# Stick-breaking attention on one core: the score products' key tile without its zero halves

## What is computed

```python
z = jnp.einsum('bqkgd,bskd->bkgqs', qb, kf)            # scores, 64 numbers a head
log_1m_beta = jnp.where(mask, jax.nn.log_sigmoid(-z), 0.0)
rev = lax.cumsum(log_1m_beta, axis=4, reverse=True)    # suffix sums over the keys
excl = jnp.concatenate([rev[..., 1:], jnp.zeros_like(rev[..., :1])], axis=-1)
a = jnp.where(mask, jnp.exp(jax.nn.log_sigmoid(z) + excl), 0.0)
o = jnp.einsum('bkgqs,bskd->bqkgd', a, vf)
```

## Time and profile before

| | us |
|---|---|
| median of 3 runs | 1886.32 |
| lowest, highest | 1879.72, 1889.54 |
| the profiled execution, its own time | 1886.43 |
| its span, first to last instruction | 1884.6 |
| PE busy | 1769.6 |
| DVE busy | 1009.6 |
| ACT busy | 864.7 |
| POOL busy | 89.9 |

### The profile page before, as it was taken

One profiled execution on the slowest core, in us unless ns is written; L12 is line 12 of the kernel. 1 busy time (PEld: TensorE's weight loads), 2 busy tenths in 40 slices (PEclk: granted clock), 3 DMA queues, 4 the chain that ended last, 5 costly groups with the idle time before them and its releaser, 6 DMA issues.

```text
span 1884.6 us, 22494 instructions
## 1 busy us (share of the span) xinstructions
PE 1769.6 (94%) x8544; PEld 1459.7 (77%) x8544; DVE 1009.6 (54%) x1351; ACT 864.7 (46%) x1221; POOL 89.9 (5%) x114
## 2 busy tenths in 40 slices
PE   7968779999997999998999999999999999799997
PEld 5758668888885688886888887888878888468886
DVE  4674536545435555545554556555455545655553
ACT  4532115543437555435443563544354444855442
POOL 0022400000011000000000100000000000000000
PEclk9989799999988999998999999999999999999999
DMA  7320005455521044554455654555545555225552
GB/s 269 151 91 1 1 24 179 178 188 190 232 91 45 23 168 178 189 201 145 178 180 204 252 181 155 180 187 190 201 162 196 182 197 198 71 90 179 178 193 97
DMA packets 41164, 291.87 MB, mean 155 GB/s; under 512 B 4832, under 2 KB 4992, under 8 KB 6528
## 3 DMA queue, kind: packets, MB, share of 16 engines
q1 hardware_dynamic: 39968, 282.91, 41.6%
q0 software_dynamic: 1120, 7.88, 1.3%
HBM read 289.73 MB, written 1.05 MB: 154 GB/s over the span
## 4 chain that ended last, share of the span: by engine, by line
PE 89%; DVE 7%; ACT 2%; issue 1%; POOL 1%; DMA 0%; SPq 0%; POOLq 0%; DVEq 0%; ACTq 0%
PE ps L577 25%; PE ps L579 25%; PE ps L578 25%; PE ps L591 3%; PE ps L1077 1%; PE ps L928 1%; DVE w_lo L1617 1%; PE ps L915 1%; PE ps L925 1%; PE ps L1006 1%; PE ps L774 1%; PE ps L1090 1%; PE ps L1103 0%; ACT w_hi L1169 0%; PE ps L956 0%
## 5 line engine op out<-in xcount | busy, mean ns | idle before, releaser
L1617 DVE TENSOR_TENSOR w_lo<-raw,w_hi 128x1024 fp32r<-128x1024 f32 (+1 forms) x532 | 619.4, 1206 | 488.9 <-ACT w_hi L1169 485.1
L1169 ACT ACTIVATE w_hi<-raw 128x1024 fp32r<-128x1024 f32 (+1 forms) x532 | 527.0, 1040 | 508.3 <-PE ps L579 496.2
L577 PE MATMUL ps<-w_hi,h_hi 128*128 128x512 f32 x1424 | 570.0, 400 | 20.7 <-DVE w_lo L1617 13.2
L579 PE MATMUL ps<-w_hi,h_lo 128*128 128x512 f32 x1424 | 560.1, 393 | 0.0
L578 PE MATMUL ps<-w_lo,h_hi 128*128 128x512 f32 x1424 | 559.4, 393 | 0.0
L577 PEld LDWEIGHTS ps<-w_hi,h_hi 128*128 128x128 f32 x1424 | 270.5, 190 | 81.9 <-issue 18.4
L579 PEld LDWEIGHTS ps<-w_hi,h_lo 128*128 128x128 f32 x1424 | 270.2, 190 | 58.3
L578 PEld LDWEIGHTS ps<-w_lo,h_hi 128*128 128x128 f32 x1424 | 271.0, 190 | 53.5
L577 PE MATMUL ps<-w_hi,hid_hi 128*128 128x512 f32 x672 | 263.2, 392 | 0.0
L579 PE MATMUL ps<-w_hi,hid_lo 128*128 128x512 f32 x672 | 261.7, 389 | 0.0
L578 PE MATMUL ps<-w_lo,hid_hi 128*128 128x512 f32 x672 | 261.5, 389 | 0.0
(11 more groups left out here) (278 smaller groups left out, 1268.8 us busy)
## 6 DMA issues: line engine op xcount, KB each, us to landing
raw<-in_stream SPq DMA_DIRECT2D x266, 1024.0 KB, 4.8
ns_w<-in_ns_w POOLq DMA_DIRECT2D x1, 4096.0 KB, 14.4
ln_rows<-in_ln_rows POOLq DMA_DIRECT2D x2, 1024.0 KB, 9.9
const<-in_const SPq DMA_DIRECT2D x1, 1202.0 KB, 14.3
x_sb<-in_x SPq DMA_DIRECT2D x2, 512.0 KB, 7.7
out<-x_sb SPq DMA_DIRECT2D x2, 512.0 KB, 3.1
row<-in_fin_rows SPq DMA_DIRECT2D x1, 512.0 KB, 18.7
row<-in_fin_rows POOLq DMA_DIRECT2D x1, 512.0 KB, 4.0
```

The lines of the kernel that those rows point to most:

```text
L577: pe.matmul(bank[tt], a_hi[:, k_at + k, rows], hi, start=(k == 0), stop=False)
L579: done = pe.matmul(bank[tt], a_lo[:, k_at + k, rows], hi, start=False, stop=(k == q.kt - 1))
L1169: act.activation(w_hi[:, static % 2, part], raw[:, static % RING, part], ACT.Copy).then_inc(hi_ready, 1)
L1617: dve.tensor_tensor(w_lo[:, static % 2, part], raw[:, static % RING, part], w_hi[:, static % 2, part].bitcast(F32), ALU.subtract).then_inc ...
```

## The change

`sb_kt` loses its `par` dimension, and with it the zeros. ACT copies all 128 partitions of the transposed keys at once; the keys stand in both halves already. The score product of `par` 0 takes rows 0 to 63 of keys and queries, that of `par` 1 rows 64 to 127. The memset, its semaphore and ACT's wait for it are gone. Results and PSUM banks are as before.

```diff
-        sb_kt = view("sb_kt", [P, 2, 4, T], 16 * KB)
+        sb_kt = view("sb_kt", [P, 4, T], 16 * KB)
...
                     for par in range(2):
-                        done = pe.matmul(ps[:, 2 * (u % 2) + par, 0:256], sb_kt[:, par, g, kt * P:(kt + 1) * P],
-                                         sb_qt[:, 2 * g:2 * g + 2, qt * P:(qt + 1) * P], start=True, stop=True)
+                        rows = slice(64 * par, 64 * par + 64)
+                        done = pe.matmul(ps[:, 2 * (u % 2) + par, 0:256], sb_kt[rows, g, kt * P:(kt + 1) * P],
+                                         sb_qt[rows, 2 * g:2 * g + 2, qt * P:(qt + 1) * P], start=True, stop=True)
...
                 def store_t(first):
 
-                    act.wait_ge(sb_kz, 1)
...
                         else:
-                            for par in range(2):
-                                rows = slice(64 * par, 64 * par + 64)
-                                done = act.activation(sb_kt[rows, par, 2 * n:2 * n + 2, :].rearrange("p f t -> p (f t)"),
-                                                      ps[rows, 4 + n % 2, :], ACT.Copy)
+                            done = act.activation(sb_kt[:, 2 * n:2 * n + 2, :].rearrange("p f t -> p (f t)"),
+                                                  ps[:, 4 + n % 2, :], ACT.Copy)
...
                     pool.tensor_copy(sb_kd[:, :, :, half, :], heads).then_inc(sb_copied, 1)
-                pool.memset(sb_kt[:, :, :, :].rearrange("p r g t -> p (r g t)"), 0.0).then_inc(sb_kz, 1)
```

More of the change, by code:

```diff
@@ L443, in build @@
         sb_copied = sem("sb_copied")
-        sb_kz = sem("sb_kz")
         sb_in = sem("sb_in")
```

## The result

| | before | after |
|---|---|---|
| median of 20 runs each, us | 1885.78 | 1889.86 |
| lowest, highest, us | 1877.35, 1889.54 | 1885.05, 1891.32 |
| ratio, 95% interval | | 1.0024 (1.0015 to 1.0033) |
| the profiled execution, us | 1886.43 | 1890.67 |
| its span, us | 1884.6 | 1888.9 |

The account below looks back on a forecast made before the run. It took TensorE, busy 94% of the span, to bound the kernel, and DVE's work the edited mixer's rounds. -1.1 us on the path plus 3.4 for the clock gave +2.3 on 1886.32: 1888.7 us, range about 1880 to 1894.

Parts of the forecast that it names:

- What goes without a price: Ahead of the mixer: removed memset wait and ACT's key copies, done 1.2 us earlier, give 0 on the path.
- The row halves: Score products on rows 0 to 63 and 64 to 127 run side by side: a unit costs 0.43 us, not 0.86.
- the step of L786: Pace of the value products on two column halves, eight records in 1.08 us, assumed for the score products.
- The rival that they don't overlap: Score products: the row halves don't run side by side; 0 to -0.5 us, about 1886 us, chance 0.10.
- The switch of shape: Array going from full to half shape at the scores: 0.14 us each in five places, 0.7 us if not hidden.
- What of it the path sees: DVE's five waits for scores in the mixer vanish: 1.1 us less; DVE is what is late next.
- What the freed time costs: PE's longer idle gaps in the mixer bring two more low-clock stretches at 1.7 us each: +3.4 us.
- The first gap: PE's idle time between the scores and the first suffix sum: 2.98 us before, 3.4 us forecast.
- one slow round for each gap over 3 us: Mixer rounds: each PE gap over 3 us brings one round at low clock; two more, 1.7 us each.
- The clock doesn't mind: Rival: PE's longer mixer gaps pass at full clock, -1.1 us remain, 1885.3 us; chance 0.30.
- Low throughout: Rival: clock stays low for the whole mixer, +11.4 us, 1897.8 us; chance 0.05.
- The 9.4 us: 0.5% of the whole kernel's time, taken as about what a measurement can tell from no change.

Follow-up runs that it names:

- filled changed kernel: The changed kernel with 5, 5, 3, 3 and 3 unread products of constants in PE's gaps ahead of the first five rounds' suffix sums: 1881.43 us, ratio 0.9967.
- filled kernel before: The kernel before with 4, 4, 2, 2 and 3 unread products of constants in PE's gaps: 1883.05 us, ratio 0.9987.
- six profiles with whole products: Profiles with full-array score product gaps: kernel before with 0, 2, 4, 6 products ahead, full-array products with new copies (1884.17 us), 64-row pairs issued twice (1886.51 us).
- four places: Either kernel with 0, 2, 4 or 6 products of constants ahead of the key transposes: before 1885.78, 1883.97, 1887.92, 1888.70 us; changed 1889.86, 1887.73, 1890.28, 1893.22 us.
- the rows alone: The kernel before with score products on 64 rows each, but par dimension, memset and four half-height copies kept: 1886.56 us, ratio 1.0006.
- the shifts: Both kernels with 2, 4 or 6 products of constants ahead of the key transposes: before 1883.97, 1887.92, 1888.70 us; changed 1887.73, 1890.28, 1893.22 us.
- the copies alone: The changed kernel with full-array score products, keeping no memset and two full-height key copies: 1884.17 us, ratio 0.9994.

## Why the prediction was right

**What goes without a price** was right by its own steps. ACT ended its key copies at 1605.2 (1605.3 worked out), waited 4.12 us for PE (3.9), and the mixer didn't come earlier.

**The row halves**: I took the step of L786, and eight records took 1.14 us where those of L786 take 1.08. The rival that they don't overlap is out. The switch of shape was priced at 0.14 us and costs about 0.2: scores start 0.96 us behind the carry sums in the filled changed kernel, 0.86 in the filled kernel before, and the first two records take 0.48 us where later ones take 0.38, which holds up the next two by 0.1. In the rounds it stayed hidden.

```profile
1644.75 0.49 PE L764 MATMUL ps<-sb_qt,sb_kt 64*128 64x256 f32 x2
```

**What of it the path sees** was named right and sized low. DVE does become the next in line: in the filled kernel, the list of its waits for 1616 to 1661 has none for scores left:

```profile
DVE sb_s L1862 <- PE ps L778: 4.1, 4, 1.0
DVE sb_s L1862 <- PE ps L776: 4.0, 8, 0.6
DVE w_lo L1624 <- ACT w_hi L1179: 0.7, 1, 0.7
```

But the gain is about 1.5 us, not 1.1. The wait list counted only DVE's idle time. A round went from 6.35 to 6.12 us, 0.23 where the wait was 0.17, in three rounds, and at the start the masking of the fourth unit came 0.77 us earlier against the transposes where the waits add up to 0.59: 1.46 in all. (The mixers' lengths differ by 1.6, because the first score product starts 0.1 us later behind the transposes, at the switch of shape.) The surplus over the waits is overlap on DVE: where the input is there, an instruction starts before the one ahead of it has ended. In the filled kernel the masking of the first round starts 0.05 us before the end of the subtraction (L1862 at 1625.88 for 0.69, masking at 1626.52), where before it came 0.17 us behind it.

**What the freed time costs** is the term that decided, and it was sized low by over a third, 3.4 us against 5.5. The first gap came out as worked out, 3.4 us. The second was 2.66 instead of 3.3, because the scores ahead of it ran at half clock, and the clock was low again all the same. So the rule that I counted by, one slow round for each gap over 3 us, picked the right two rounds without being the right rule: the second and third slow rounds followed 2.66 and 2.02 us. Its premise, that gaps of 2.98 and 2.64 us pass, came from one execution; in the six profiles with whole products they were followed by slow sums in half the cases. I took two more slow rounds at 1.7 us; there were three more, and two of them made DVE wait 0.5 us for its scores besides. The chain after has, for the scores of a round's first unit at half and at full clock, and for the carry sums of the last slow round:

```profile
1627.97 1.18 PE ps L764 x4
...
1635.70 1.18 PE ps L764 x4
...
1644.82 0.66 PE ps L764 x4
...
1660.71 0.94 PE ps L776 x2
```

The sum: L774 over 1.98 us by 1.80, 1.08, 1.62 and 1.64, L776 by 0.07, the first unit's scores of two rounds by 0.5 each over 0.66, is 7.2 us; less the 1.7 of the slow round before, 5.5; less the 1.5 won, 4.0. Measured between the two traces, from the second block's transposes to the end of the mixer: 4.1 us. The forecast's form, minus the path gain plus the clock, is right, with -1.5 and +5.5 in place of -1.1 and +3.4. That 1888.7 came so near to 1889.9 is in part luck: the errors of the two terms went opposite ways, and the count of slow rounds differs from one execution to the next, from one to three in the kernel before and from three to four in the changed one at its four places.

**Rivals.** "The clock doesn't mind" is out. "Low throughout" didn't happen: after each slow round of the profiled run the clock came back. The 9.4 us named as what a measurement can tell from no change was far too coarse: 20 runs of each tell 4.1 us from nothing. The Trainium skill (TensorE: Matmul & The Clock Gate, section What's actually happening) calls the lower rate the default, which activity lifts; what filling did agrees, with a granted clock of 1.00 from 1619.6 us on. The Trainium skill (TensorEngine Tiling (Array Packing), section Key Properties) says that a change of tiling mode drains the array; the rows show some 0.2 us at the switch, which nothing waited for in the rounds.

Not shown: what decides between a gap of 2.05 us that passes and one of 2.02 us that doesn't; why the rows alone, with the same products, are mostly some 3 us faster than the changed kernel; and why the profiled run and the median differ at the shifts.

## What to carry to other kernels

Before taking work off an engine that waits for others within its stage, ask what its clock does in the gaps: here TensorE gave up 0.75 us of work a round, most of it work that nobody waited for, and paid up to 1.8 us on the suffix sums that everybody waits for. Don't read from one execution which gaps the clock lets pass: here the same gaps passed in some and not in others. A saving off the path is worth its overlap with another engine's wait and no more, and that can be read ahead of time in the wait list (1.1 us here, about 1.5 in truth). Where such gaps are short and fixed, products of constants in them are a cheap test of whether the clock is what one pays for, and here also gave the fastest version measured.

## What the runs showed of the hardware that I had not expected

- With nothing changed in its own work, the mixer of the kernel before took 47.2 to 50.4 us, through one to three slow rounds, and 51.8 in the kernel with the copies alone. Each is one execution. Of the profiles taken at the shifts, a pair could have shown the changed mixer anything from 1.2 us shorter (49.2 against 50.4) to 4.3 longer (51.5 against 47.2).
- A gap of 2.02 us on PE was followed by half clock and one of 2.05 us wasn't. The same gap of 2.98 us ahead of the first suffix sums was followed by sums at full clock in two profiles and by slow ones in three, with as much work of PE ahead of it in the mixer. So the length of the last gap alone doesn't tell.
- Two f32 products on the two row halves start together although each is two records of the same half in a row. At half clock a record of L764 took 0.63 us before and the next started 0.43 us behind it, so that two in a row span 1.06 us; after the change the first two span 0.80. Together they still take 0.17 us longer than one did before, the price of the switch of shape in it. The trace doesn't name the half that a record uses; that a pair is one of each half is inferred from the rows before, where the two records of a product never start together. All records of the line in the kernel before (least, median, longest ns) and two in a row there:

```profile
L764 PE MATMUL ps<-sb_qt,sb_kt x48: 379/379/634, 1616.4 to 1649.0; 128*128 128x256 f32 x48
1616.78 1.06 PE L764 MATMUL ps<-sb_qt,sb_kt 128*128 128x256 f32 x2
```

The first two in the changed kernel:

```profile
1616.59 0.80 PE L764 MATMUL ps<-sb_qt,sb_kt 64*128 64x256 f32 x2
```
